# Room between the blocks of four stationary tiles in the expert stage

## The reference

```python
logits = jnp.dot(xt, w_r)                       # 320 x 8
top_v, top_i = lax.top_k(logits, 2)
gates = softmax(top_v) spread over the 8 experts
for e in range(8):
    h = jax.nn.silu(xt @ wg[e]) * (xt @ wu[e])  # 1024 -> 3584
    y = y + gates[:, e:e+1] * (h @ wd[e])       # 3584 -> 1024
```

## The kernel before

| tile | start before, mod 512 | distance of its blocks |
|---|---|---|
| `split_hi`, `split_lo` (streams, 2048 bytes each) | 320 | 2048 |
| `xgT_hi`, `xgT_lo` | 64, 64 | 512 |
| `hmT_hi`, `hmT_lo` | 320, 64 | 512 |
| `cut_hi`, `cut_lo` (stationary, first part) | 128 | 512 |
| `xT_hi` (stream of 1280 bytes) | 320 for even blocks, 64 for odd | 1280 |
| `xT_lo` (stream) | 128 for even blocks, 384 for odd | 1280 |
| `hT_hi`, `hT_lo` (streams) | 96 and 352 in turn | 1280 |

## Time and profile before

### The profile page before, as it was taken

The page is one execution under the profiler, slowest core; times in us unless marked ns, Lnnn a source line. Parts: engine busy times, 40 slices in busy tenths (PEclk is TensorE's granted clock), DMA queues, the critical chain, the costliest instruction groups (busy, mean ns, idle before and its releaser), DMA issues.

```text
span 1535.8 us, 21611 instructions
## 1 busy us (share of the span) xinstructions
PE 1527.8 (99%) x8428; PEld 1333.0 (87%) x8428; DVE 1234.4 (80%) x1253; ACT 998.9 (65%) x1079; POOL 217.5 (14%) x249
## 2 busy tenths in 40 slices
PE   9999999999999999999999999999999999999998
PEld 7989999999998988888888888888888888888887
DVE  5877666654477758988988888998998988898897
ACT  5655433333466547777777778777777777777775
POOL 5514400001150403101001001002002002002000
PEclk9999999999999999999999999999999999999999
DMA  8333455444443459999999999999999999999994
GB/s 226 96 110 116 149 164 164 133 157 151 125 122 110 141 209 367 383 366 388 372 381 376 374 374 376 391 359 386 384 363 382 381 362 379 400 361 363 394 373 183
DMA packets 159701, 437.43 MB, mean 285 GB/s; under 512 B 12068, under 2 KB 66176, under 8 KB 145264
## 3 DMA queue, kind: packets, MB, share of 16 engines
q1 hardware_dynamic: 151796, 423.02, 75.0%
q0 software_dynamic: 5552, 9.62, 2.3%
q10 hardware_dynamic: 2252, 3.41, 0.7%
HBM read 429.40 MB, written 13.60 MB: 288 GB/s over the span
## 4 chain that ended last, share of the span: by engine, by line
PE 98%; DMA 0%; ACT 0%; DVE 0%; issue 0%; SPq 0%; DVEq 0%; ACTq 0%
PE bank L1981 34%; PE bank L2475 13%; PE bank L2484 13%; PE bank L2479 13%; PE bank L2510 6%; PE bank L2513 6%; PE bank L2519 6%; PE bank L1984 3%; PE bank L2528 2%; PE bank L2496 0%; PE bank L2502 0%; PE bank L2495 0%; DMA gla<-b_g 0%; DVE x L1972 0%; ACT L1076 0%
## 5 line engine op out<-in xcount | busy, mean ns | idle before, releaser
L1808 DVE TENSOR_TENSOR split_lo<-raw,split_hi 128x2048 fp32r<-128x2048 f32 x336 | 763.1, 2289 | 101.8 <-ACT split_hi L1207 100.8
L1207 ACT CAST split_hi<-raw 128x2048 fp32r<-128x2048 f32 x336 | 640.5, 1911 | 224.5 <-PE bank L2484 145.7
L2475 PE MATMUL bank<-split_hi,xgT_hi 128*128 128x512 f32 x896 | 291.7, 395 | 0.0
L2479 PE MATMUL bank<-split_hi,xgT_lo 128*128 128x512 f32 x892 | 285.8, 390 | 0.0
L2484 PE MATMUL bank<-split_lo,xgT_hi 128*128 128x512 f32 x896 | 239.9, 390 | 0.0
L913 ACT CAST cut_hi<-ring 128x1024 fp32r<-128x1024 f32 x124 | 129.9, 1048 | 166.6 <-PE bank L1981 166.6
L1981 PE MATMUL bank<-xT_hi,cut_hi 128*128 128x320 f32 x752 | 236.7, 315 | 0.0
L1981 PE MATMUL bank<-xT_hi,cut_lo 128*128 128x320 f32 x752 | 233.5, 310 | 0.0
L1981 PE MATMUL bank<-xT_lo,cut_hi 128*128 128x320 f32 x752 | 231.9, 308 | 0.0
L1346 DVE TENSOR_TENSOR cut_lo<-ring,cut_hi 128x1024 fp32r<-128x1024 f32 x124 | 153.0, 1235 | 80.7 <-ACT cut_hi L913 79.9
L2484 PEld LDWEIGHTS bank<-split_lo,xgT_hi 128*128 128x128 f32 x896 | 168.3, 188 | 34.9
(11 more groups left out here) (316 smaller groups left out, 1723.2 us busy)
## 6 DMA issues: line engine op xcount, KB each, us to landing
raw<-moe_w_gate SPq DMA_DIRECT2D x112, 1024.0 KB, 7.8
raw<-moe_w_up SPq DMA_DIRECT2D x112, 1024.0 KB, 7.6
raw<-moe_w_down SPq DMA_DIRECT2D x112, 1024.0 KB, 7.3
ring<-w_in SPq DMA_DIRECT2D x15, 1024.0 KB, 5.5
ring<-ffn_w_gate SPq DMA_DIRECT2D x11, 1024.0 KB, 5.5
ring<-ffn_w_up SPq DMA_DIRECT2D x11, 1024.0 KB, 5.4
ring<-ffn_w_down SPq DMA_DIRECT2D x10, 1024.0 KB, 5.1
ring<-w_out SPq DMA_DIRECT2D x8, 1024.0 KB, 5.0
```

Of the source, the lines that this page charges most:

```text
L1207: return nc.scalar.copy(split_hi[:, i % SR, :], raw_piece(i)).then_inc(hi_ready, 1)
L1808: V.tensor_tensor(split_lo[:, i % SR, :], raw_piece(i), split_hi[:, i % SR, :].bitcast(F32), ALU.subtract).then_inc(lo_ready, 1)
L2475: TE.matmul(o, xgT_hi[:, kk, :], hi[:, w * k + 512 * c:w * k + 512 * c + 512], start=kk == 0, stop=False)
L2479: TE.matmul(o, xgT_lo[:, kk, :], hi[:, w * k + 512 * c:w * k + 512 * c + 512], start=False, stop=False)
```

## The change

Each of the four tiles is given some words of room behind each block of 128: 8 words in `xgT_hi`, 12 in `xgT_lo`, 4 in `hmT_hi`, 20 in `hmT_lo`. The blocks' distances become 544, 560, 528 and 592 bytes. An unused tile of 16 words behind `hmT_hi` makes its growth 512 bytes (28 x 16 + 64), so that `ye`, `hm`, `split_hi` and `split_lo` move by one block length and keep their offsets modulo 512. Every matmul reads the same number of words in the same order as before. The two writers of `hmT_hi` and `hmT_lo` now write four blocks of 128 with a gap between instead of 512 words in a row, and DVE reads `hmT_hi` the same way. The writers of `xgT_hi` and `xgT_lo` write one block at a time as before. The streams' and the first part's tiles that the table names have the offsets that they had; `xg`, `hs`, `Gown`, `last_hot` and small tiles behind the four move along.

```diff
+XH_W, XL_W, HH_W, HL_W = P + 8, P + 12, P + 4, P + 20
-        hmT_hi = sb("hmT_hi", [P, FEB, P], FR)
+        hmT_hi = sb("hmT_hi", [P, FEB, HH_W], FR)[:, :, 0:P]
+        sb("beyond_hmT_hi", [P, 16])
-        xgT_hi = sb("xgT_hi", [P, KB, P], FR)
-        xgT_lo = sb("xgT_lo", [P, KB, P], FR)
+        xgT_hi_room = sb("xgT_hi", [P, KB, XH_W], FR)
+        xgT_hi = xgT_hi_room[:, :, 0:P]
+        xgT_lo_room = sb("xgT_lo", [P, KB, XL_W], FR)
+        xgT_lo = xgT_lo_room[:, :, 0:P]
-        hmT_lo = sb("hmT_lo", [P, FEB, P], FR, loop_only)
+        hmT_lo = sb("hmT_lo", [P, FEB, HL_W], FR, loop_only)[:, :, 0:P]
-        last_y_hi = xgT_hi[:].rearrange("p k n -> p (k n)")
-        last_y_lo = xgT_lo[:].rearrange("p k n -> p (k n)")
+        last_y_hi = xgT_hi_room[:].rearrange("p k n -> p (k n)")[:, 0:D]
+        last_y_lo = xgT_lo_room[:].rearrange("p k n -> p (k n)")[:, 0:D]
...
-  nc.scalar.copy(hmT_hi[:, 4 * j:4 * j + 4, :].rearrange("p b n -> p (b n)"), tb[n % 2][:]).then_inc(th_ready, 1)
+  nc.scalar.copy(hmT_hi[:, 4 * j:4 * j + 4, :], tb[n % 2][:].rearrange("p (b n) -> p b n", b=4)).then_inc(th_ready, 1)
...
-  V.tensor_tensor(hmT_lo[:, 4 * j:4 * j + 4, :].rearrange("p b n -> p (b n)"), tb[n % 2][:],
-                  hmT_hi[:, 4 * j:4 * j + 4, :].rearrange("p b n -> p (b n)").bitcast(F32), ALU.subtract).then_inc(t_free, 1)
+  V.tensor_tensor(hmT_lo[:, 4 * j:4 * j + 4, :], tb[n % 2][:].rearrange("p (b n) -> p b n", b=4),
+                  hmT_hi[:, 4 * j:4 * j + 4, :].bitcast(F32), ALU.subtract).then_inc(t_free, 1)
```

## The result

The changed kernel takes 1554.82 us (median of 4, 1553.94 to 1557.06), the kernel before in the same session 1536.62 us. The ratio is 1.0118, with a 95% interval of 1.0106 to 1.0130: 18 us slower, where 6 us faster was forecast, and outside the stated range. The profiled execution spans 1555.3 us against 1535.8.

A forecast was written before the change was run, and what follows sets the result against it. PE's pitch over 4032 large matmuls, 226.7 ns against 213.3 of streaming, was taken as the bound. Saving 1.5 ns each, 6.0 us, brings the span from 1535.8 to 1529.8; plus 1.1 gives 1531 us, range 1520 to 1543.

The forecast's parts named there:

- Nearest to the new state is the `xT` stretch: First part's `xT` matmuls, saving 1.2 ns, taken as model for expert matmuls: 1.5 ns each, 6.0 us faster.
- None of the steady stretches lies above 13.4: Across the trace's steady matmul stretches, the time added to the stream's own was said never to exceed 13.4 ns.
- The slower rival: Expert stage: changing offsets keep PE from settling at 226.7 ns; up to 4.7 ns x 4032 = 19 us, 1556; chance 0.19.
- the matmuls after transposes: Expert stage: seven matmuls after transposes take 231.4 ns, 4.7 above the settled pitch; used to size a possible 19 us loss.

The follow-up runs named there:

- shift8: All four stationary tiles of the kernel before start 32 bytes later, no room between blocks: 1562.97 against 1538.27 us, ratio 1.0169.
- streams8: Only `split_hi` and `split_lo` start 32 bytes later than in the kernel before, stationary tiles unmoved: 1560.84 against 1538.31 us, ratio 1.0142.
- first0: In the kernel before, first-part streams `hT` moved 8 words and `xT_hi` 16, to distance 0: 1541.03 against 1538.69 us, ratio 1.0009.
- hT56: In the kernel before, only the first part's `hT` streams moved 56 words, to distance 64 bytes: 1541.0 us in one run.
- room64: Room of 64 words (256 bytes) behind every block of all four stationary tiles of the kernel before: 1538.95 against 1538.27 us, ratio 1.0006.
- lo60: Only `xgT_lo` and `hmT_lo` start 60 words (240 bytes) later than in the kernel before: 1539.85 against 1538.69 us, ratio 1.0007.
- shift16: All four stationary tiles of the kernel before start 16 words (64 bytes) later, streams unmoved: 1562.06 against 1538.31 us, ratio 1.0154.
- lo16: Only `xgT_lo` and `hmT_lo` start 16 words (64 bytes) later than in the kernel before: 1555.57 against 1538.84 us, ratio 1.0109.
- both8: Streams and all four stationary tiles start 8 words (32 bytes) later than in the kernel before: 1539.53 against 1538.31 us, ratio 1.0006.

## Why the prediction was wrong

**Right:** PE's pitch in the expert stage is the only thing that moves (the chain, the waits, 4017 against 4097 in the windows); the first part stays, 895 and 527 matmuls; the writers and the loads cost nothing. That the addresses of two operands matter at all was read rightly from the trace of before, and shift8 and streams8 bear it out. The Trainium skill ("SBUF — State Buffer", the section Who interferes with whom) has the weight load and the stream on read ports that are independent, by which the time would have stayed; the runs disagree, with 22 to 26 us for 32 bytes on either side.

**The step that failed** is the size and sign in "Nearest to the new state is the `xT` stretch ... I take 1.5 ns". In its place the runs measured +4.8 ns a matmul. The stretch was the wrong neighbour in two ways. It has streams of 320 words, for which constant distances of 0, 32 and 64 all give 146.7 ns (first0, before, hT56), while in the expert stage, at 512 words, the same three give 227.1, 233.2 and 233.2. And what I took as a second witness, that 0 and 256 modulo 512 both gave 226.7 in the expert stage, was one point: the two are the same distance modulo 256. The sentence "None of the steady stretches lies above 13.4" was true of the means of whole stretches, and only because none with 512 words was at any distance but this one. Inside the `xT` stretch it was not true: the odd blocks' 147.3 ns on average, which the prediction put at 146.7, are 0.6 more than `hT` has, and the even ones' 143.8 are 2.8 less, where it had 2.1. So there was a small sign in the trace that an offset can be dear as well. The trace of before held no measurement of the new layout at 512 words, and I should have given the unseen values the larger share.

**The slower rival** had 0.19, and its 1556 us came within 1.2 us of the result. That was mostly luck, since its place was wrong. It held that evenly laid blocks let PE settle, so that changing ones would cost; but blocks that change by 256 bytes are free (room64), as are tiles at 0 and 240 (lo60), while blocks that never change are dear at 32 to 128 bytes, and are settled there, at 231 and 236 ns in turn (shift16). That the matmuls after transposes had 231.4 ns was a coincidence of size, as far as the runs go.

**How the 4.8 ns add up.** An even mixture of all sixteen distances that are multiples of 16, from the seven measured and straight lines between them, has a mean of 230.8 ns. Weighted by how often each tile of the changed kernel has each distance, it is 230.9. These are estimates from the table above. They account for 3.7 or 3.8 of the 4.8 ns. The rest has not been traced; lo16 shows that mixtures can cost more than their parts, and a price of large changes of distance would be in that rest.

**Still open** is the mechanism. That moving both sides together is free (both8) suggests two reads of one memory that get in each other's way by address; no run shows how, or why the curve has its shape. Why the first part is indifferent is not explained either: its streams are shorter, but no run changed the length alone, and its stationary tiles and their order differ too.

No version beats the kernel before. lo60, with the lowest mean pitch (227.0), ties with it.

## What to carry to other kernels

Where each fp32r matmul of 512 words has a weight load beside it, try laying stationary blocks and streams so that their starts differ by a multiple of 256 bytes. In this kernel, the only one measured, that is worth up to 1.7% of the time, and the one distance tried off the multiples of 16 bytes, 248, costs as much as the worst. What counts is the difference, so one pad ahead of one tile mends it, and a pad of 256 bytes between blocks does no harm. And a stretch with another shape is no witness for it: before relying on a neighbour in the trace, ask whether it has the same shape, and whether the values that agree are truly different values.

## What the runs showed of the hardware that I had not expected

- The pitch of fp32r matmuls of 128x512 with a load each depends on the distance between stationary block and stream modulo 256 bytes: 227.1 ns at 0, 229.6 at 16, 233.2 at 32 and 64, 232.3 at 128, 229.0 at 192, 227.9 at 240.
- It depends on nothing else of the two places that was tried: both 32 bytes on, 227.1 ns; blocks 256 bytes further apart, 227.1 ns.
- With only the lo tiles at 64 bytes, matmuls with a hi block in use and a hi block next go from 226.9 to 230.6 ns.
- At 248 bytes, off the multiples of 16, it is 233.3 ns.
- For the 128x320 of the first part it is 146.7 ns at distances 0, 32 and 64, and 145.4 where hi streams are at 64 and lo streams at 0; there even blocks have a mean of 143.8 and odd ones of 147.3, at equal distances modulo 256.
- A copy to four blocks of 128 words with gaps takes ACT the 579 ns and DVE within 2 ns of the 684 that 512 words in a row take.
